# Padding two places of the SBUF layout of a one-core transformer kernel, so that stage buffers start at other addresses

## The reference

```python
def swiglu(x, w_gate, w_up, w_down):
    return (jax.nn.silu(x @ w_gate) * (x @ w_up)) @ w_down
...
x = x + 0.5 * swiglu(rms_norm(x, g_ffn1[l]), ...)                            # ffn0
x = x + jnp.concatenate([y_attn, y_conv, y_mem], axis=-1) @ w_out[l]         # mixA, outA
x = x + 0.5 * swiglu(rms_norm(x, g_ffn2[l]), ...)                            # ffn1
...
y = _dsa_mixer(h, ...)            # second model, layer 0: mixB, outB, then ffn2
y = _short_conv_mixer(h, ...)     # second model, layer 1: mixC, outC, then ffn3
```

## The kernel before

| tensor | start | rest by 64 |
|---|---|---|
| h_hi, h_lo | 32896, 49280 | 0, 0 |
| w_hi, w_lo | 82048, 98432 | 0, 0 |
| wi, the last kept (32 columns) | 138976 | 32 |
| hid_hi, hid_lo | 139104, 184160 | 32, 32 |
| outA_lo, outA_hi | 142176, 158560 | 32, 32 |
| mh_hi, mh_lo | 158560, 166752 | 32, 32 |
| raw2_hi, raw2_lo | 196448, 212832 | 32, 32 |
| qA, kA, qB, kB, qi, ki | 174944, 183136, 142176, 158560, 166816, 175008 | 32 |
| mq, mk (behind vA, 520 columns) | 187264, 191360 | 0, 0 |
| zc (1028 columns, so 4112 bytes), c_sb, tap | 139104, 143232, 147328 | 32, 0, 0 |
| y_hi, y_lo | 151424, 167808 | 0, 0 |

## Time and profile before

### The profile page before, as it was taken

The page is one execution under the profiler, slowest core; times in us unless marked ns, Lnnn a source line. Parts: engine busy times, 40 slices in busy tenths (PEclk is TensorE's granted clock), DMA queues, the critical chain, the costliest instruction groups (busy, mean ns, idle before and its releaser), DMA issues.

```text
span 2206.7 us, 28945 instructions
## 1 busy us (share of the span) xinstructions
PE 2160.9 (98%) x10222; PEld 1763.4 (80%) x10226; DVE 1212.3 (55%) x1760; ACT 783.4 (35%) x1081; POOL 234.3 (11%) x237
## 2 busy tenths in 40 slices
PE   7999999899999999999989999999999999999999
PEld 6888888687888888877767888888888878888887
DVE  6655444695565554455787475553456457333332
ACT  5222233446542223333445342222333224222221
POOL 0000200560200020013210200000000000000000
PEclk8999999999999999999989999999999999999999
DMA  4665233320245542333210135552332222222232
GB/s 160 197 188 182 90 92 100 110 93 20 86 134 182 188 155 79 91 104 101 87 48 1 67 117 187 181 171 76 91 109 96 102 89 87 95 95 95 78 95 83
DMA packets 75733, 242.96 MB, mean 110 GB/s; under 512 B 9328, under 2 KB 9584, under 8 KB 75536
## 3 DMA queue, kind: packets, MB, share of 16 engines
q1 hardware_dynamic: 61376, 189.61, 26.5%
q0 software_dynamic: 14288, 52.44, 7.7%
HBM read 235.65 MB, written 2.10 MB: 108 GB/s over the span
## 4 chain that ended last, share of the span: by engine, by line
PE 90%; DVE 7%; ACT 1%; issue 1%; DMA 0%; ACTq 0%; SPq 0%; DVEq 0%
PE ps L659 27%; PE ps L661 27%; PE ps L660 27%; PE ps L967 2%; PE ps L925 1%; PE ps L946 1%; PE ps L745 1%; DVE tmp L1564 1%; DVE score L1982 1%; DVE h_lo L1593 1%; DVE top L1980 1%; PE ps L928 1%; DVE tmp L1585 0%; PE ps L1092 0%; DVE w_lo L1521 0%
## 5 line engine op out<-in xcount | busy, mean ns | idle before, releaser
L659 PE MATMUL ps<-h_hi,w_hi 128*128 128x512 f32 x1888 | 746.8, 396 | 17.1 <-issue 8.1
L661 PE MATMUL ps<-h_hi,w_lo 128*128 128x512 f32 x1888 | 738.7, 391 | 0.0
L660 PE MATMUL ps<-h_lo,w_hi 128*128 128x512 f32 x1888 | 738.2, 391 | 0.0
L1521 DVE TENSOR_TENSOR w_lo<-w_raw,w_hi 128x1024 fp32r<-128x1024 f32 x336 | 413.2, 1231 | 439.6 <-ACT w_hi L1173 429.0
L1173 ACT ACTIVATE w_hi<-w_raw 128x1024 fp32r<-128x1024 f32 x383 | 402.6, 1052 | 257.4 <-PE ps L661 256.0
L659 PEld LDWEIGHTS ps<-h_hi,w_hi 128*128 128x128 f32 x1888 | 356.0, 189 | 99.6 <-issue 19.7
L661 PEld LDWEIGHTS ps<-h_hi,w_lo 128*128 128x128 f32 x1888 | 355.5, 188 | 76.5
L660 PEld LDWEIGHTS ps<-h_lo,w_hi 128*128 128x128 f32 x1888 | 356.2, 189 | 73.1
L659 PE MATMUL ps<-hid_hi,w_hi 128*128 128x512 f32 x704 | 278.4, 396 | 0.0
L660 PE MATMUL ps<-hid_lo,w_hi 128*128 128x512 f32 x704 | 278.4, 396 | 0.0
L661 PE MATMUL ps<-hid_hi,w_lo 128*128 128x512 f32 x704 | 278.4, 396 | 0.0
(11 more groups left out here) (303 smaller groups left out, 1749.3 us busy)
## 6 DMA issues: line engine op xcount, KB each, us to landing
ada_raw<-in_ada_w POOLq DMA_DIRECT2D x96, 512.0 KB, 4.2
w_raw<-in_gate SPq DMA_DIRECT2D x88, 512.0 KB, 3.5
w_raw<-in_up SPq DMA_DIRECT2D x88, 512.0 KB, 3.5
w_raw<-in_down SPq DMA_DIRECT2D x64, 384.0 KB, 3.0
w_raw<-in_down SPq DMA_DIRECT2D x64, 320.0 KB, 2.8
w_raw<-in_w_mix_c SPq DMA_DIRECT2D x24, 512.0 KB, 3.5
w_raw<-in_w_mix_b SPq DMA_DIRECT2D x17, 512.0 KB, 3.5
w_raw<-in_w_mix SPq DMA_DIRECT2D x16, 512.0 KB, 3.5
```

Source lines behind the costliest of these rows:

```text
L659: pe.matmul(dest, s_hi, m_hi, start=first and n == 0, stop=False)
L660: pe.matmul(dest, s_hi, m_lo, start=False, stop=False)
L661: mm = pe.matmul(dest, s_lo, m_hi, start=False, stop=last and n == len(pairs) - 1)
L1521: dve.tensor_tensor(chunk(w_lo, slot, WT), chunk(w_raw, slot, WT), f32(chunk(w_hi, slot, WT)), ALU.subtract).then_inc(w_lo_done, 1)
```

## The change

Two tensors are added that nothing reads or writes. `to_line`, 22 columns, is the last kept tensor, so that it moves the start of every stage set. `roomC`, 12 columns, stands between `zc` and `c_sb` in the set of mixC and outC. No instruction is added, removed or reordered; only addresses change.

```diff
@@ -119,6 +119,7 @@
         qinv = keep("qinv", 8 * 8)
         wi = keep("wi", TT * 8)
+        keep("to_line", 22)
         ps = ctx.enter_context(nc.psum_tensor("ps", [P, 8 * T], F32))
@@ -146,8 +147,8 @@
-        zc, c_sb, tap, y_hi, y_lo = stage_memory([
-            ("zc", 2 * (PAD_B + T), F32), ("c_sb", 2 * T, F32), ("tap", 2 * T, F32), ("y_hi", KC * T, F32R),
+        zc, _, c_sb, tap, y_hi, y_lo = stage_memory([
+            ("zc", 2 * (PAD_B + T), F32), ("roomC", 12, F32), ("c_sb", 2 * T, F32), ("tap", 2 * T, F32), ("y_hi", KC * T, F32R),
             ("y_lo", KC * T, F32R)])
```

## The result

The changed kernel takes 2199.71 us (median of 20, 2193.28 to 2208.83), the kernel before 2209.78 us (median of 20, 2201.59 to 2214.55). The ratio is 0.9961 with a 95% interval of 0.9949 to 0.9972, so it gains 8.6 us (6.2 to 11.3). The forecast was a gain of 14.1 us and 2191 us: right in sign, too large by two thirds, and the time lies just above the range. On another chip the same kernel had the ratio 0.9951 (0.9932 to 0.9970).

The account below looks back on a forecast made before the run. TensorE's own stream was taken to bound the kernel. The terms summed to -14.1 us, from a median of 2204.99 us to 2190.9, predicted as 2191 us; its own range was 2186 to 2195, for all cases 2185 to 2199.

Parts of the forecast that it names:

- What bounds the kernel: Whole kernel: TensorE, busy 98% of the span, sets the time; shortening the distance between a stream's matmuls shortens the program.
- the chance of 0.79 to 64 bytes: Main forecast, chance 0.79: moving buffers starting at multiples of 64 bytes are enough for the fast step, 226.7 ns.
- Term 1: Four down stages, 2112 matmuls: -14.04 us, together -13.7 us after 0.31 us waited away at ffn1's end.
- Term 2: outA's closed stream of 167 matmuls: -1.1 us; nothing taken for the 25 before it.
- Term 3: raw2, 48 matmuls of which 25 run closed: -0.2 us, between 0 and -0.3.
- Term 4: mh, 3 x 32 matmuls of 256 columns: half the long stream's gain each, -0.3 us (0 to -0.6).
- Term 5: y, 184 matmuls of a closed stream going from rest 0 to 32: +1.2 us; lower end 0.
- Terms 6 and 7: Plain float32 operands (keys, queries, transposes): 0, with 0.6 us kept for the range; other engines' accesses to hid: no gain.
- the first: Rival: starts must be multiples of more than 64 bytes; full form, no gain and y loses 1.2, 2206.2 us, chance 0.09.
- its half form: Rival: hid's start at 64 by 128 costs half as much as before; about 2198.6 us, chance 0.05.
- The second: Rival: the start isn't what counts, something else hid and outA share does; nothing moves, 2205.0 us, chance 0.03.
- The clock: Rival: mixB's attention shifts on stretches of low TensorE clock and the kernel gets slower, about 2212 us, chance 0.04.

Follow-up runs that it names:

- m2: Own kernel without the computation: float32r streams of 48 matmuls with fewer stationary or 256 moving columns, by distance; 8 stationary columns: 226.8 ns at 0, 231.7 at 32.
- m1: Own kernel without the computation: streams of 48 matmuls at each moving-to-stationary distance, three data types; float32r 226.7 ns at 0, 233.3 at 32 bytes.
- e1: Against the kernel before, pads put hid, outA, raw2, mh and y all at multiples of 128 bytes; 2192.37 us against 2206.89, ratio 0.9918.

## Why the prediction was wrong in size

- **What bounds the kernel**: right. TensorE's stream sets the time in the down stages, nothing hides a gain there, and what the streams gained is what the kernel gained.
- **The step that failed** is the sentence "Every long stream at rest 0 steps by 226.7 ns and every one at rest 32 by 233.3 ns", read as a rule on the moving start by 64 bytes and carried over to hid at 139200. The rows held only two distances from the weights, 0 and 224. The start's rest and the distance were one and the same in them, since the weights never moved; I didn't list the stationary operand as a candidate. What held the chance of 0.79 to 64 bytes was a count of cycles (544, one more for each piece of 64 bytes); hid starts at a multiple of 64 now and takes 228.9 x 2.4 = 549, so that count was no evidence. The runs put in its place: the distance of the moving from the stationary start by 256 bytes counts, and 64, where the change puts hid, costs 228.9 ns.
- **Term 1, down stages**: forecast -13.7 us. Measured 2112 x (233.3 - 228.9) = -9.3 us. The idle time of PE at ffn1's end went from 0.81 to 0.86 us and not to 1.1. The 47 matmuls there gained 0.21 us in place of 0.31, and the chain on VectorE took 0.16 us less, counted from the same ScalarE split to PE's next start.
- **Term 2, outA**: -1.1 forecast, 167 x 4.4 = -0.7 measured. **Term 3, raw2**: -0.2 forecast, -0.1 measured, with steps of 228.8 ns.
- **Term 4, mh**: -0.3 forecast. Its closed streams of 24 go from 2.80 us between first and last start to 2.79: 0.0. m2 shows why a half of the long stream's price was no estimate: 256 columns have an order of their own.
- **Term 5, y**: the sign, against the change's name, was right; +1.2 forecast, 179 x 7.4 = +1.3 measured.
- **Terms 6 and 7**: right. But the 428 ns that `mk,mq` and `ki,qi` of 64x256 had and keep are mean durations, which don't say how fast a stream runs, so term 6 was right on weak evidence. It is m1 that shows it, with records of plain float32 429.2 ns apart at each of its three distances; ScalarE's and VectorE's times into hid didn't move (632 and 693 ns).
- The sum of the measured terms is -9.3 - 0.7 - 0.1 + 1.3 = -8.8 us, and the timing has -8.6 (6.2 to 11.3). Nothing else is needed.
- **The rivals**: the first was nearest in time, its half form gave 2198.6 us, but not in mechanism: multiples of 128 didn't make y fast in e1. The second was right that the start by itself isn't what counts, and wrong in its price of nothing: what hid and outA shared was their distance from the weights. The bfloat16 streams of m1 run at 215.8 ns at every distance tried, and the float32r ones don't. The Trainium skill (page "TensorE: Matmul & The Clock Gate", section "Back-to-back issue gap") has 215.8 ns for 512 columns by its formula, which it calls the gap of an isolated matmul, and about 131 ns for a stream of weight loads and matmuls. m1's bfloat16 stream loads weights for each matmul and agrees with the formula; no stream here comes near 131 ns, and the formula doesn't cover the float32r streams. The clock didn't turn the sign, though it moves single executions by several microseconds.

**What stays open.** Why the distance matters. m2 excludes that the loss is in proportion to the weight columns read, and also that distance 0 is best for every shape. Even the best float32r stream stays at 226.7 ns, 11 above the bfloat16 stream's 215.8 ns, and no distance tried gave less. The distance by 256 isn't all of it either: at distance 128 the same stream takes 232.4 ns in e1, 232.7 in m1 and 233.3 in m2. No run tried a low half at another rest than its high half.

## What to carry to other kernels

In a stream of float32r matmuls with 128 stationary and 512 moving columns, put the moving buffers a multiple of 256 bytes from the weight buffers, counted between the two and not from the partition's start; between starts at multiples of 32 bytes it is worth up to 7.6 ns in 234. For bfloat16 or plain float32 don't bother, and for other shapes measure: with 256 moving columns a multiple of 256 bytes was the slowest choice tried. When a table of cases shows that a price follows an address, ask what else was constant in it: move the other operand once before believing the rule. And count starts from the allocator's own rounding, since padding by the sum of columns moved y away from where it was meant to go.

## What the runs showed of the hardware that was not expected

- A float32r stream of 128x512 steps by 226.7 ns at distance 0 or -16 bytes from the stationary operand, 228.9 at 64, 233.3 at 32, 192 and 224, 233.3 to 233.5 at 96, 232.4 to 233.3 at 128 and 234.2 at 160. The same stream in bfloat16 steps by 215.8 ns at all seven distances tried. In plain float32 it has two records for each matmul, 429.2 ns apart, at all three.
- Moving the weights by 32 bytes while h stayed (e4) slowed the long streams on h from 226.7 to 233.3 ns; the one execution took 37.7 us, 1.7%, more than the median before, of which the h streams explain some 34.
- Loading 8 stationary columns in place of 128 left the step at distance 0 at 226.8 ns (m2).
- With 256 moving columns distance 0 is the slowest of five: 119.8 ns, and 117.9 ns at 32 (m2).
